# Six projection blocks of the HGRN mixer as seven half products each, their weight quarters added by accumulating DMAs

## The reference, cut to what matters

```python
proj = (u @ w_in).astype(f32)                       # u: 512 x 1024, w_in: 1024 x 12320
(hq, hf, hi, hg, gq, gk, gv, ga, gb, gz, gate_h, gate_g) = jnp.split(proj, offsets, axis=-1)
log_f = jnp.logaddexp(jnp.log(lb), jnp.log1p(-lb) + jax.nn.log_sigmoid(hf))
k_h = -jnp.expm1(log_f)
q_h = jax.nn.silu(hq) * HG_DK ** -0.5
o_h = hgrn2_chunked(q_h, k_h, hi, log_f)            # 8 heads, chunks of 64 tokens
o_h = rmsnorm(o_h, hgrn_out_norm) * jax.nn.silu(hg)
y_h = o_h @ w_branch_hgrn
y = jax.nn.sigmoid(gate_h) * y_h + jax.nn.sigmoid(gate_g) * y_g
```

## Time and profile before

| | us |
|---|---|
| median of 3 runs | 2761.47 |
| lowest, highest | 2759.97, 2762.94 |
| the profiled execution | 2757.06 |
| its span, first to last instruction | 2755.3 |
| TensorE busy in it | 2692.9 |
| VectorE, ScalarE busy | 1260.5, 638.4 |

### The profile page before, as it was taken

The page is one execution under the profiler, slowest core; times in us unless marked ns, Lnnn a source line. Parts: engine busy times, 40 slices in busy tenths (PEclk is TensorE's granted clock), DMA queues, the critical chain, the costliest instruction groups (busy, mean ns, idle before and its releaser), DMA issues.

```text
span 2755.3 us, 29095 instructions
## 1 busy us (share of the span) xinstructions
PE 2692.9 (98%) x11586; PEld 1802.2 (65%) x11586; DVE 1260.5 (46%) x2498; ACT 638.4 (23%) x1460; POOL 59.6 (2%) x115
## 2 busy tenths in 40 slices
PE   8999899999999999999999999999999999999999
PEld 4445557656468888746556755656565685688886
DVE  5733333444234456425363426464654451344564
ACT  2123221246200000132342122434242202000001
POOL 0000000000000000000000001010110000000000
PEclk9999999999999999999999999999999999999999
DMA  4211012100122222220110131121111321222222
GB/s 154 82 41 62 31 63 80 62 31 1 61 92 92 84 72 89 77 92 31 62 61 31 63 122 40 53 77 47 62 47 62 145 92 61 92 92 91 73 82 77
DMA packets 121439, 194.91 MB, mean 71 GB/s; under 512 B 6172, under 2 KB 62296, under 8 KB 120408
## 3 DMA queue, kind: packets, MB, share of 16 engines
q1 hardware_dynamic: 119888, 180.95, 19.3%
q0 software_dynamic: 1296, 12.06, 1.1%
q10 hardware_dynamic: 120, 0.03, 0.0%
HBM read 185.69 MB, written 7.34 MB: 70 GB/s over the span
## 4 chain that ended last, share of the span: by engine, by line
PE 95%; DVE 2%; ACT 1%; DMA 1%; issue 1%; ACTq 0%; DVEq 0%; SPq 0%
PE psum L507 19%; PE psum L504 14%; PE psum L2260 14%; PE psum L417 9%; PE psum L437 8%; PE psum L2242 8%; PE psum L402 6%; PE psum L1140 2%; PE psum L2123 2%; PE psum L1160 2%; PE psum L635 1%; PE psum L390 1%; PE psum L1148 1%; PE psum L2471 1%; PE psum L2337 1%
## 5 line engine op out<-in xcount | busy, mean ns | idle before, releaser
L2260 PE MATMUL psum<-weight_ring,h_t 128*128 128x512 f32 x896 | 407.4, 598 | 0.5 <-issue 0.5
L560 DVE TENSOR_TENSOR arena<-arena,psum 128x512 f32<-128x512 f32 x179 | 122.8, 686 | 336.8 <-PE psum L507 287.6
L2260 PEld LDWEIGHTS psum<-weight_ring,h_t 128*128 128x128 f32 x896 | 162.7, 191 | 162.0 <-issue 160.8
L417 PE MATMUL psum<-h_t,weight_ring 128*128 128x512 f32 x544 | 237.2, 597 | 6.7 <-DMA weight_ring<-in_w_in_dram 4.8
L2242 PE MATMUL psum<-h_t,weight_ring 128*128 128x512 f32 x512 | 235.3, 602 | 1.7 <-ACT arena L2646 1.4
L507 PE MATMUL psum<-h_t,weight_ring 128*128 128x256 f32 x1024 | 228.2, 380 | 0.0
L504 PE MATMUL psum<-weight_ring,arena 128*128 128x256 f32 x992 | 220.2, 380 | 1.5 <-ACT arena L2683 1.5
L507 PEld LDWEIGHTS psum<-h_t,weight_ring 128*128 128x128 f32 x1024 | 195.1, 191 | 26.9 <-issue 1.3
L504 PEld LDWEIGHTS psum<-weight_ring,arena 128*128 128x128 f32 x992 | 189.0, 191 | 27.1 <-issue 2.2
L417 PEld LDWEIGHTS psum<-h_t,weight_ring 128*128 128x128 f32 x544 | 103.7, 192 | 136.0 <-issue 129.1
L402 PE MATMUL psum<-weight_ring,h_t 128*128 128x512 f32 (+2 forms) x448 | 172.1, 543 | 0.8 <-DVEq L1605 0.8
(11 more groups left out here) (405 smaller groups left out, 3294.7 us busy)
## 6 DMA issues: line engine op xcount, KB each, us to landing
weight_ring<-in_ffn_w_in_dram SPq DMA_DIRECT2D x44, 1024.0 KB, 6.8
weight_ring<-in_w_in_dram SPq DMA_DIRECT2D x20, 2048.0 KB, 7.8
weight_ring<-in_ffn_w_out_dram SPq DMA_DIRECT2D x8, 2048.0 KB, 7.9
weight_ring<-in_w_in_even_dram SPq DMA_DIRECT2D x7, 2048.0 KB, 8.0
weight_ring<-in_w_in_odd_dram SPq DMA_DIRECT2D x5, 2048.0 KB, 7.9
weight_ring<-in_w_in_dram SPq DMA_DIRECT2D x8, 1024.0 KB, 6.6
weight_ring<-in_w_branch_gdn_dram SPq DMA_DIRECT2D x4, 2048.0 KB, 8.9
weight_ring<-in_ffn_w_out_dram SPq DMA_DIRECT2D x4, 1536.0 KB, 6.8
```

What stands on the lines that cost most here:

```text
L417: last = pe.matmul(bank, slot[:, k, c:c + P], act[:, k, :], start=(k == 0), stop=(k == KD - 1))
L560: ins = dve.tensor_tensor(out, other, bank, op)
L2260: last = pe.matmul(bank, act[:, k, t * P:(t + 1) * P], slot[:, k, :], start=(k == 0), stop=(k == KD - 1))
```

## The change

**Which blocks.** hq 0, hi 0, hg 0, hq 1, gate_h 0 and gate_h 1 are now seven half products each (`pe_seven_streamed`), in the order p4, p1, p2, p5, p6, p7, p3. hi 1, hg 1, hf 0 and hf 1 stay plain.

**Sums of weights.** They have no buffers. GpSimd issues accumulating DMAs that add one quarter of the block into another in its ring slot, 512 KB each in runs of 1 KB: w21 += w11 once the block has landed; after p4 w22 += w12, read from DRAM; after p1 w11 += w22; after p2 w12 += w11. Each of the last three waits for the one before. p5, p6 and p3 wait for the first, second and third of the chain, p7 for the difference. `weights_used` now rises at p2, the third product.

**Sums of tokens.** One set serves all six blocks, since their tokens are the same. It lies in `x_res`, whose content (the residual) is copied to DRAM by GpSimd before and copied back after the last streamed product. VectorE makes the set before it takes up hf 0.

**Adding up.** ScalarE copies p4, p1 and p5 out with the sign turned, VectorE does the rest in seven steps of 128 x 512 (`dve_streamed`). Silu and Sigmoid come later, on whole arrays.

**Places.** In g = 0, three products of hi stand before the levels, and then 2, 2, 2, 2, 2, 1, 0 after each round (`HGRN_UNITS`). A filler block gives four products before the keys, one before the hu of head 3 and two after them. gate_h 1 gives four before the transposes and three after. In the state section the work has banks 0 to 4 and the streams 5 to 7.

```diff
+LOW_FIVE, HIGH_THREE = tuple(range(BANKS - 3)), tuple(range(BANKS - 3, BANKS))
...
+STREAMED = ("p4", "p1", "p2", "p5", "p6", "p7", "p3")
+SUMMED = {"p5": 1, "p6": 2, "p3": 3}
+
+
+def pe_seven_streamed(K, pe, key, act, tokens, token_major, among=None):
+
+    blk = K.next_block()
+    n = KD // 2
+    w11, w12, w21, w22 = quarters(K, blk, KD)
+    t1, t2, t4, t3 = sums_view(tokens, KD)
+    x11, x21, x22 = act[:, 0:n, LOW], act[:, n:KD, LOW], act[:, n:KD, HIGH]
+    sides = {"p4": (w22, t4), "p1": (w11, x11), "p7": (w21, t3), "p2": (w12, x21), "p5": (w22, t1), "p6": (w11, t2),
+             "p3": (w12, x22)}
+    K.streamed_at[key[1:]] = blk, K.count("blocks_streamed")
+    at = K.streamed_at[key[1:]][1]
+    pe.wait_ge(K.weight_landed[blk % SLOTS], K.landed_at[blk])
+    for name in STREAMED:
+        left, right = sides[name]
+        bank = K.next_bank((key, name), among)
+        if K.turn((key, name)) > 1:
+            pe.wait_ge(K.free_of((key, name)), K.turn((key, name)) - 1)
+        if name == "p7":
+            pe.wait_ge(K.difference_landed, 16 * at)
+        if name in SUMMED:
+            pe.wait_ge(K.chain_landed, 48 * (at - 1) + 16 * SUMMED[name])
+        for q in range(2):
+            for k in range(n):
+                out, first, last = bank[:, q * HALF:(q + 1) * HALF], k == 0, k == n - 1
+                if token_major:
+                    ins = pe.matmul(out, right[:, k, q * P:(q + 1) * P], left[:, k, :], start=first, stop=last)
+                else:
+                    ins = pe.matmul(out, left[:, k, q * P:(q + 1) * P], right[:, k, :], start=first, stop=last)
+                if name == "p2" and q == k == 0:
+                    ins.then_inc(K.weights_used, 1)
+        ins.then_inc(K.full_of((key, name)), 1)
+        yield
+
+
+def pool_quarter_sums(K, pool, key):
+
+    blk, at = K.streamed_at[key[1:]]
+    w11, w12, w21, w22 = quarters(K, blk, KD)
+    (_, src), = K.blocks[blk]
+    pool.wait_ge(K.weight_landed[blk % SLOTS], K.landed_at[blk])
+    pool.dma_start(w21, w11, accum_op=ALU.add).then_inc(K.difference_landed, 16)
+    pool.wait_ge(K.full_of((key, "p4")), K.turn((key, "p4")))
+    pool.dma_start(w22, src[:, 0:KD // 2, HALF:2 * HALF], accum_op=ALU.add).then_inc(K.chain_landed, 16)
+    pool.wait_ge(K.full_of((key, "p1")), K.turn((key, "p1")))
+    pool.wait_ge(K.difference_landed, 16 * at)
+    pool.wait_ge(K.chain_landed, 48 * at - 32)
+    pool.dma_start(w11, w22, accum_op=ALU.add).then_inc(K.chain_landed, 16)
+    pool.wait_ge(K.full_of((key, "p2")), K.turn((key, "p2")))
+    pool.wait_ge(K.chain_landed, 48 * at - 16)
+    pool.dma_start(w12, w11, accum_op=ALU.add).then_inc(K.chain_landed, 16)
+
+
+def dve_streamed_tokens(K, dve, act, tokens):
+
+    n = KD // 2
+    t1, t2, t4, t3 = sums_view(tokens, KD)
+    x11, x12, x21, x22 = act[:, 0:n, LOW], act[:, 0:n, HIGH], act[:, n:KD, LOW], act[:, n:KD, HIGH]
+    dve.tensor_tensor(t1, x11, x12, ALU.subtract).then_inc(K.one_more("dve"), 1)
+    dve.wait_ge(K.steps["dve"], K.step_n["dve"])
+    dve.tensor_tensor(t2, x22, t1, ALU.add).then_inc(K.one_more("dve"), 1)
+    dve.tensor_tensor(t3, x22, x12, ALU.subtract).then_inc(K.one_more("dve"), 1)
+    dve.wait_ge(K.steps["dve"], K.step_n["dve"])
+    dve.tensor_tensor(t4, t2, x21, ALU.subtract).then_inc(K.tokens_summed, 1)
+
+
+def act_streamed(K, act, key, name, quarter, base):
+
+    n = K.streamed_at[key[1:]][1]
+    out = {"p4": quarter(1, 0), "p1": base, "p5": quarter(1, 1)}[name]
+    key = (key, name)
+    act.wait_ge(K.full_of(key), K.turn(key))
+    if n > 2 and name == "p1":
+        act.wait_ge(K.base_done, n - 2)
+    bank = pair(K.bank(key)) if len(out.shape) == 3 else K.bank(key)
+    act.activation(out, bank, ACT.Copy, scale=-1.0).then_inc(K.free_of(key), 1)
+
+
+def dve_streamed(K, dve, key, name, quarter, base):
+
+    c11, c12, c21, c22 = (quarter(c, t) for c, t in ((0, 0), (0, 1), (1, 0), (1, 1)))
+    at = (key, name)
+    if name == "p2":
+        dve.wait_ge(K.free_of((key, "p1")), K.turn((key, "p1")))
+        dve.wait_ge(K.full_of(at), K.turn(at))
+        dve.tensor_tensor(c11, pair(K.bank(at)), pair(base), ALU.subtract).then_inc(K.free_of(at), 1)
+        dve.wait_ge(K.free_of(at), K.turn(at))
+    if name == "p6":
+        dve_product(K, dve, key, "p6", base, base)
+    if name == "p7":
+        dve_product(K, dve, key, "p7", c12, pair(base), ALU.subtract)
+        dve.wait_ge(K.free_of((key, "p5")), K.turn((key, "p5")))
+        dve.tensor_tensor(base, base, c22, ALU.add).then_inc(K.one_more("dve"), 1)
+        dve.wait_ge(K.steps["dve"], K.step_n["dve"])
+        dve.tensor_tensor(c22, c22, c12, ALU.add).then_inc(K.one_more("dve"), 1)
+        dve.wait_ge(K.free_of((key, "p4")), K.turn((key, "p4")))
+        dve_add(K, dve, c21, c12)
+    if name == "p3":
+        dve.wait_ge(K.full_of(at), K.turn(at))
+        dve.tensor_tensor(c12, pair(K.bank(at)), pair(base), ALU.subtract).then_inc(K.free_of(at), 1)
+        dve.wait_ge(K.free_of(at), K.turn(at))
+        dve.tensor_copy(K.stat[:, 76:77], K.stat[:, 77:78]).then_inc(K.base_done, 1)
...
-    blk = K.next_block()
-    pe.wait_ge(K.weight_landed[blk % SLOTS], K.landed_at[blk])
-    pe_feature_major(K, pe, (s, "hq", 0), K.h_t, [0, P, 2 * P, 3 * P], blk)
+    K.token_sums["pe"] += 1
+    pe.wait_ge(K.tokens_summed, K.token_sums["pe"])
+    pe_take(pe_seven_streamed(K, pe, (s, "hq", 0), K.h_t, V["tokens_s"], False), 7)
+        if g == 0:
+            inner = pe_hgrn_stream(K, pe, s, V)
+            pe_take(inner, HGRN_UNITS[0])
+        else:
+            blk = K.next_block()
+            pe.wait_ge(K.weight_landed[blk % SLOTS], K.landed_at[blk])
+            pe_token_major(K, pe, (s, "hi", g), K.h_t, 512, blk=blk, tiles=HGRN_FIRST)
...
+            if g == 0:
+                pe_take(inner, HGRN_UNITS[lv + 1])
+            elif lv < len(HGRN_REST):
...
-            fill = pe_stream_feature(K, pe, (s, "hq", 1), K.h_t)
+            fill = pe_seven_streamed(K, pe, (s, "hq", 1), K.h_t, V["tokens_s"], False, HIGH_THREE)
         else:
-            fill = pe_stream_token(K, pe, (s, "gate_h", 0), K.h_t)
-        pe_take(fill, 2 * KD)
+            fill = pe_seven_streamed(K, pe, (s, "gate_h", 0), K.h_t, V["tokens_s"], True, HIGH_THREE)
+        pe_take(fill, 4)
...
-            fill = pe_stream_token(K, pe, (s, "gate_h", 1), K.h_t)
-            pe_take(fill, 2 * KD)
+            fill = pe_seven_streamed(K, pe, (s, "gate_h", 1), K.h_t, V["tokens_s"], True, HIGH_THREE)
+            pe_take(fill, 4)
...
-    pe_take(fill, 2 * KD)
+    pe_take(fill, 3)
...
+HGRN_UNITS = (3, 2, 2, 2, 2, 2, 1, 0)
+HGRN_FIRST = (0, 1, 2)
+HGRN_REST = (("hi", 3), ("hg", 0), ("hg", 1), ("hg", 2), ("hg", 3))
...
-    K.banks_in_turn = WORK_BANKS
+    K.banks_in_turn = LOW_FIVE
...
-            pe_take(fill, KD)
+            pe_take(fill, 1)
...
-    pe_take(fill, KD)
+    pe_take(fill, 2)
...
+HGRN_COPIES = ((("hi", "p4"), ("hi", "p1")), (("hi", "p5"),), (), (("hg", "p4"), ("hg", "p1")), (("hg", "p5"),), (), (), ())
+HGRN_SUMS = {0: (("hi", "p2"),), 1: (("hi", "p6"),), 2: (("hi", "p7"), ("hi", "p3")), 4: (("hg", "p2"),),
+             5: (("hg", "p6"), ("hg", "p7")), 6: (("hg", "p3"),)}
...
+        beside = ("gate_h", 0) if g else ("hq", 1)
+        act_hgrn_part(K, act, s, V, *beside, "p4")
         act.drain().then_inc(K.phase_met, 1)
         act.wait_ge(K.phase_met, K.phase_end("act"))
+        act_hgrn_part(K, act, s, V, *beside, "p1")
...
+        act_hgrn_part(K, act, s, V, *beside, "p5")
...
+    dve.wait_ge(K.x_spilled, 16)
+    dve_streamed_tokens(K, dve, K.h_t, V["tokens_s"])
...
+        if g == 0:
+            dve_hgrn_sums(K, dve, s, V, "hq", 0, "p2", "p6", "p7", "p3")
+        dve.wait_ge(K.hgrn_queries, 1 + g)
...
+        beside = ("gate_h", 0) if g else ("hq", 1)
+        dve_hgrn_sums(K, dve, s, V, *beside, "p2")
...
+        dve_hgrn_sums(K, dve, s, V, *beside, "p6", "p7", "p3")
...
+    dve_hgrn_sums(K, dve, s, V, "gate_h", 1, "p2")
     for kt in range(KD):
         dve.wait_ge(K.free_of((s, "o_t", kt)), K.turn((s, "o_t", kt)))
     dve_token_sums(K, dve, V["o_t"], KD, V["tokens0"])
-    for half in range(2):
-        dve_weight_sums(K, dve, K.branch_blocks["y_h"] + half, KD, V[f"weights{half}"], None)
+    dve_hgrn_sums(K, dve, s, V, "gate_h", 1, "p6")
+    dve_weight_sums(K, dve, K.branch_blocks["y_h"], KD, V["weights0"], None)
+    dve_hgrn_sums(K, dve, s, V, "gate_h", 1, "p7", "p3")
+    dve_weight_sums(K, dve, K.branch_blocks["y_h"] + 1, KD, V["weights1"], None)
...
+def pool_hgrn(K, pool, s):
+    pool.wait_ge(K.lb_shifted, 1)
+    pool.dma_start(K.x_dram, K.x_res[:]).then_inc(K.x_spilled, 16)
+    for name, g in HGRN_BASES:
+        pool_quarter_sums(K, pool, (s, name, g))
+    last = ((s, "gate_h", 1), "p3")
+    pool.wait_ge(K.full_of(last), K.turn(last))
+    pool.wait_ge(K.x_spilled, 16)
+    pool.dma_start(K.x_res[:], K.x_dram).then_inc(K.x_reloaded, 16)
```

(1 more changed line is left out.)

86 lines of the change are left out of this document (55 added, 31 removed).

## The result

The changed kernel took 2772.38 us at the median (2767.12 to 2786.77, 20 runs), beside 2764.39 for the kernel before (2756.45 to 2779.93, 20 runs). The ratio is 1.0033, with a 95% interval of 1.0019 to 1.0047: slower by a third of a per cent, some 9 us. The time lies in the stated range, but the forecast had said 5 us faster.

The account below looks back on a forecast made before the run. TensorE's multiplying was taken as the bound: 11.8 us of waits plus 2.6 of DMA wait minus 19.8 saved gives -5.4, so 2756.0 us against the median 2761.47. The range leaving two in ten out was 2751.5 to 2775.

Parts of the forecast that it names:

- the stated range: Whole kernel: the range that leaves two in ten out, from 2751.5 to 2775 us.
- The saving: Six streamed blocks on TensorE: seven half products replace a whole block, 3.30 us saved each, 19.8 us together.
- Waits by buffers and order: TensorE at hq 1, keys, sixth hu product and gate_h 1 with y_h: new waits, together 11.8 us.
- What only moves: VectorE and ScalarE steps, x's copies and weight loads: added or shifted work hidden by slack, costing nothing.
- lost in full: TensorE in the HGRN part: each new wait costs its length, since nothing idles beside it.
- The chain of DMAs: Three dependent accumulating DMAs per block: only a 2.6 us wait, at p6 of hq 0.
- L = 6: Accumulating DMAs: 6 us from the end of the awaited product to landing; 7 for the second of hq 0.
- The limits of the prediction for two sums: p6: 10.35 us for two chained DMAs in hq 0; scores give 3.6 or 7.1 more in hi and hg.
- The prediction's own sign of being wrong: Accumulating DMAs landing in over 7.5 us; also TensorE waiting at p5, or the hu wait missing.
- "chain slow" rival: Each sum takes 8.5 us or more, first at p5 and p6 of hq 0; price 17 us at 8.5; chance 0.24.
- -5.4: Whole change: 11.8 us of bank and order waits plus 2.6 of DMA wait minus 19.8 saved.
- L near 8.8: Upper end of the range, 2775 us: time from the awaited product's end to a DMA's landing near 8.8 us.

Follow-up runs that it names:

- the last kernel: Changed kernel, all six blocks streamed, with filler product before sixth hu product, p7 before p6, p1's copy and p2's step later, rotation shifted: 2743.20 us, ratio 0.9915.
- no_chain: The changed kernel without its 24 accumulating DMAs and TensorE's waits on them, so weight quarters are not added: ratio 0.9979 to the kernel before.

## Why the prediction was wrong

Held, by its own steps:
- **The saving.** Half products stood at 3.455 us each, 24.2 for seven, and -14.25 in the last kernel, beside 4.1 us of waits, needs more than the 16.5 of five blocks.
- **Waits by buffers and order.** All four places were there: +0.65 at the first product of hq 1 (0.7 said), 0.16 and 1.58 before the keys (0.3, 1.5), 2.93 and 2.94 before the sixth hu product (3.0 each), 1.82 before p6 of gate_h 1 with 0.31 among the transposes ahead of it (2.2). Only the first product of y_h waited 0.59 and not 1.1, of which 0.2 was a slip in the sum: 1542.5 and twice 0.8 are 1544.1, not 1544.3. In sum 11.0 against 11.8.
- **What only moves.** VectorE did not become late in the levels, x's copies and the later loads hid.

Failed:
- **A wait was priced as its length.** This is the larger part. The prediction took each new wait of TensorE as "lost in full", that is at +3.0 for each hu wait and +2.6 for hq 0, and no more. Behind the hu waits come 3.1 and 2.8 us of slow clock and 0.5 each of restart, behind the DMA wait of hq 0 2.2: 9.1 us that no term held. The rows could not show it, since the part had clock 1.00 throughout; but for the same reason it had no wait to read a price from. Its nearest row stood right behind it, in the timeline of the kernel before:

```profile
1607.41 29.30 PE L417 MATMUL psum<-h_t,weight_ring 128*128 128x512 f32 x64 [4.81 <-DMA weight_ring<-in_w_in_dram]
```

  That is the wait of the earlier trace rows and 1.7 us more than the 27.6 that such a block takes elsewhere. The price is not clean there, since gab's narrow products had lowered the clock to 0.72 before the wait, but it was a warning, and the prediction made no use of it.
- **The chain of DMAs**, priced at +2.6, measured 4.74 + 4.04. The size of a single sum was right (6.0 from DRAM, 5.4 to 5.7 in the ring; L = 6 was taken). The step that failed is that only the second sum of hq 0 was given the company of a load, and at 1 us. `weights_used` rises at p2 in every block, so the second sum of each block meets the next load: 8.0 to 8.5 us in four blocks, 9.1 in hi, 12.6 in hg (6.7 there with the load moved). The limits of the prediction for two sums, 13.9 in hi (10.35 and 3.6) and 17.4 in hg (10.35 and 7.1), held; the sums came 2.0 us behind each. The prediction's own sign of being wrong, a landing in over 7.5, is this one. It also adds up unlike the prediction's "chain slow" rival: nothing at p5, where it should have begun, all at p6.

With both, -5.4 becomes -5.4 + 9.1 + 6.2 - 0.8 = +9.1 for the stretch; 11.03 were measured, so 1.9 stay unassigned, 0.2 to 0.6 in each of the stages that stream. Of these, the 0.7 of hq 0 and the levels went with the DMA waits in no_chain. The gain of 2.35 at gqk 0 was not foreseen either and hides part of the loss.

That the time lies in the stated range is luck: the upper part of the range was made for a slow chain, L near 8.8, which would have given some 20 us by DMAs alone. The loss came about without it: 6.9 of the 9.1 us lie behind two waits that had been foreseen to a tenth of a microsecond.

## What to carry to other kernels

Where an engine with a gated clock is busy all the time, a new wait of 3 to 5 us cost its length and about 2 to 4 us more here; so a saving of 3 us per block should first be spent on keeping other work ready in front of the late buffer, as one moved line did here for 12 us. A chain of dependent DMAs has to be priced with everything that the change itself makes start beside it, in each block and not only in the tightest. When products are added to a rotation of buffers, look at who meets whom for the rest of the part.
